# Turned attention exponents moved between quadrants: through a DRAM scratch with 5 transfers a step, or from SBUF to SBUF with 16

## Chip, cores and metric

One core of one Trainium2 chip. The metric is the time of one launch of the kernel on the device, in microseconds, as the median of several runs; smaller is better.

## The reference

Two layers over 512 latent tokens of width 2048, with 256 context tokens and adaptive normalisation. The change lies in the attention of the first layer: 12 query heads in 4 groups of 3 (one key/value head each), windows of 128 tokens on either side, the context in front, and a sink logit per head.

```python
def attend_block(args):                      # one block n of 128 queries
    n, qn = args
    kw = lax.dynamic_slice_in_dim(kp, n * BLOCK, BLOCK + 2 * WINDOW, axis=1)
    vw = lax.dynamic_slice_in_dim(vp, n * BLOCK, BLOCK + 2 * WINDOW, axis=1)
    s_win = jnp.einsum('bqkgd,bjkd->bkgqj', qn, kw).astype(jnp.float32) * scale
    s_ctx = jnp.einsum('bqkgd,bjkd->bkgqj', qn, k_ctx).astype(jnp.float32) * scale
...
    logits = jnp.concatenate([sink_logits(sink, s_win.shape[:-1]), s_ctx, s_win], axis=-1)
    p = jax.nn.softmax(logits, axis=-1)
...
    return (jnp.einsum('bkgqj,bjkd->bqkgd', p_ctx, v_ctx)
            + jnp.einsum('bkgqj,bjkd->bqkgd', p_win, vw))
```

The second product needs the probabilities with the keys on the partitions, while the first leaves the queries there. So each 128 x 128 tile of exponents has to be transposed.

## The kernel before

All products are made of three passes: both operands are split in a high part (`_hi`, made by ScalarE, ACT) and the rest (`_lo`, made by VectorE, DVE), and `three` multiplies high by high, high by low and low by high on TensorE (PE). Every matmul has line 1578, and every weight unit (512 KB, 128 x 1024) is loaded by SyncE's queue (SP, `load`, line 383), split by ACT (line 543) and DVE (line 972) and then used by PE in four banks.

**Attention.** For each of the 4 key/value heads (called heads 0 to 3 below) `attention(i)` on each engine runs through 16 slots; slots 0 to 11 hold a step k each: one query head over one block of 128 queries (block n = k // 3, query head k % 3). A step is 128 x 512 exponents for the first and last block, 128 x 640 for the others. The order on each engine is written out by hand and is that of the program:

- PE: `scores(i, k)` (it waits for `negmax_ready`, the row minimum of the step before, and in the first step of a block for the pieces of the queries), then two or three fillers, quarters of a weight unit of the gate projection; in slots 6, 9, 12 and 15 also `attend(i, n)`, the product with the values, which waits for `pt_ready` of the block's three steps.
- DVE in slot k: `maximum` (line 1265, masks the scores and takes the row minimum), `piece` (line 1238, `q_lo` for the next block's queries in slots 2, 5, 8), `turned_lo` of step k - 4 (line 1288), `turn_blocks` (line 1275), the sums' reciprocals, `lo` of a weight unit, `block_out` (line 1296, the block's values times the inverse sums, in slots 6, 9, 12, 15), and in heads 0 and 1 parts of a rotation (lines 1061 to 1065).
- ACT: `exponent` (line 744), `hi` of a weight unit, `turned_hi` of step k - 3 (line 754).
- Step 0 of heads 1 to 3 runs in slot 14 of the head before.

**The transpose.** `turn_blocks` transposes 32 x 32 blocks in place with one DVE instruction, from `probs` into one of two buffers `blocks_out` (the two parts of `cond_row`). What is left is to move blocks between the four quadrants of 32 partitions: the piece at quadrant a, quarter j has to go to quadrant j, quarter a. The SP queue does it in two trips: `store_blocks` (line 422) writes the 128 rows into the DRAM tensor `blocks`, and `fetch_blocks` (line 431) waits for that (`written`) and for a free landing buffer (`pt_ready`), and reads it back with 4 transfers, one per destination quadrant, into one of three landing buffers `blocks_in` (in `cond_row` and `modchunk`). The fetch of step k - 1 stands behind the store of step k in the queue. `turn_blocks` of step g overwrites the buffer of step g - 2, so it waits for `written` of that step:

```python
if g >= 2:
    dve.wait_ge(written[g % 2], 16 * (g // 2))
```

`turned_hi` waits for the landing of the four fetches (`pt_landed`, 64 a step).

The inverse sums of a block (128 x 3) go by `store_inverse` (line 438) to DRAM and come back broadcast over the partitions by `fetch_inverse` (line 445), 192 KB in SBUF, into one of two buffers; the fetch stands in slot 3 n + 3 and waits for `y_done` of two blocks before.

GpSimd's queue (POOL) loads in the earlier stages chunks of another weight (line 489) into `modchunk`, which is free in the attention; in the attention it only waits: its next instruction (line 519) needs the last `pt_ready`.

## Time and profile before

| | us |
|---|---|
| median of 3 runs | 1404.65 |
| lowest, highest | 1404.41, 1405.91 |
| the profiled execution | 1405.84 |
| its span | 1404.1 |
| TensorE matmul busy | 1367.9 (97%) |
| VectorE busy | 864.5 (62%) |
| ScalarE busy | 517.5 (37%) |
| GpSimd busy | 74.8 (5%) |
| mean granted TensorE clock | 0.999 |

A row of a timeline gives the start from the span's start, the duration, engine, line, operation, the names written and read, the shape, and in brackets the time for which the engine was idle before it with what ended that idle time. DMA instructions show the time that the issuing queue took, not the transfer; the time to landing is listed on its own. The attention lies from 385 to 646 us of the span.

### The profile page before, as it was taken

How to read it: one execution, taken by the hardware profiler on the slowest of the kernel's cores; microseconds unless marked ns; L12 is line 12 of the kernel's file. 1: busy time of each engine (PE TensorE's matmuls, PEld its weight loads, DVE VectorE, ACT ScalarE, POOL GpSimd, SP SyncE). 2: the span in 40 equal slices, each digit the busy share in tenths (PEclk: the TensorE clock that was granted, in tenths of full speed). 3: DMA queues.
4: the chain of work that ended last, by engine and by line, in shares of the span. 5: the costliest groups of instructions: out<-in, count | busy, mean ns of one | idle time of the engine just before them, and what ended most of it. 6: DMA issues, size and time to landing. Idle time of an engine off the chain costs nothing.

```text
span 1404.1 us, 19111 instructions
## 1 busy us (share of the span) xinstructions
PE 1367.9 (97%) x7258; PEld 1142.4 (81%) x7258; DVE 864.5 (62%) x1327; ACT 517.5 (37%) x798; POOL 74.8 (5%) x145
## 2 busy tenths in 40 slices
PE   5999999999999999999999999999999999999998
PEld 2788888888878788878888888888888888887887
DVE  6545655656787787776645776677665334474435
ACT  5323422234564645454222442212363223333332
POOL 0001111111000000000110100000000000010000
PEclk9999999999999999999999999999999999999999
DMA  9996567666676757687766666356533333365333
GB/s 384 407 396 250 180 206 254 191 186 198 201 208 163 192 172 178 176 230 261 236 198 192 195 192 194 92 173 195 160 91 102 103 91 105 105 198 181 111 90 120
DMA packets 103490, 265.35 MB, mean 189 GB/s; under 512 B 13536, under 2 KB 41200, under 8 KB 102000
## 3 DMA queue, kind: packets, MB, share of 16 engines
q1 hardware_dynamic: 81792, 185.72, 42.5%
q0 software_dynamic: 19936, 73.38, 16.7%
q10 hardware_dynamic: 1680, 5.10, 1.0%
q8 instruction: 57, 0.93, 0.3%
q14 instruction: 25, 0.20, 0.1%
HBM read 245.78 MB, written 18.38 MB: 188 GB/s over the span
## 4 chain that ended last, share of the span: by engine, by line
PE 83%; DMA 6%; DVE 5%; issue 2%; SPq 2%; ACT 2%; DVEq 0%; ACTq 0%
PE ps L1578 83%; DMA blocks<-cond_row 2%; DMA modchunk<-blocks 2%; DMA kvmem<-in_ctxT 1%; SPq L431 1%; DVE w_lo L972 1%; DVE pt_lo L1288 1%; DMA raw<-in_mod 1%; ACT w_hi L543 1%; DVE cond_row L1275 1%; DVE tmp L1265 0%; SPq L389 0%; DVE tmp L1098 0%; DVE kvmem L1160 0%; DVE kvmem L1265 0%
## 5 line engine op out<-in xcount | busy, mean ns | idle before, releaser
L1578 PE MATMUL ps<-h_hi,w_hi 128*128 128x512 f32 x1592 | 621.0, 390 | 2.1 <-DVE h_lo L1053 1.2
L1578 PE MATMUL ps<-h_lo,w_hi 128*128 128x512 f32 x1592 | 618.5, 389 | 0.0
L1578 PE MATMUL ps<-h_hi,w_lo 128*128 128x512 f32 x1592 | 618.2, 388 | 0.0
L972 DVE TENSOR_TENSOR w_lo<-raw,w_hi 128x1024 fp32r<-128x1024 f32 x206 | 252.2, 1224 | 371.2 <-ACT w_hi L543 370.3
L543 ACT CAST w_hi<-raw 128x1024 fp32r<-128x1024 f32 x206 | 216.1, 1049 | 598.8 <-PE ps L1578 598.7
L1578 PEld LDWEIGHTS ps<-h_hi,w_hi 128*128 128x128 f32 x1592 | 299.0, 188 | 65.8 <-issue 5.4
L1578 PEld LDWEIGHTS ps<-h_hi,w_lo 128*128 128x128 f32 x1592 | 298.9, 188 | 62.0
L1578 PEld LDWEIGHTS ps<-h_lo,w_hi 128*128 128x128 f32 x1592 | 299.0, 188 | 58.5
L978 DVE CUSTOM_DVE_ANT_0 modchunk<-modchunk,cond_row 128x1024 f32<-128x1024 f32 x128 | 154.6, 1219 | 19.9 <-DMA modchunk<-in_modb 19.7
L489 POOL DMA_DIRECT2D modchunk<-in_modb x128 | 67.6, 528 | 828.3 <-DVE modacc L978 811.9
L744 ACT ACTIVATE tmp<-tmp,stat 128x513 f32<-128x513 f32 (+1 forms) x24 | 18.7, 780 | 43.1 <-DVE stat L1265 43.0
L1578 PE MATMUL ps<-raw,kvmem 128*32 128x128 f32 x512 | 18.8, 293 | 15.9 <-DMA raw<-in_mod 15.7
L1578 PE MATMUL ps<-pt_hi,v_hi 128*128 128x384 f32 x72 | 25.2, 350 | 9.3 <-DVE pt_lo L1288 9.3
L1578 PE MATMUL ps<-k_hi,q_hi 128*128 128x256 f32 (+1 forms) x96 | 28.8, 300 | 2.2 <-DVE q_lo L1238 2.1
L1578 PEld LDWEIGHTS ps<-raw,kvmem 128*32 128x32 f32 x512 | 14.0, 116 | 19.8 <-issue 16.1
L744 ACT ACTIVATE kvmem<-kvmem,stat 128x513 f32<-128x513 f32 (+1 forms) x24 | 18.7, 779 | 29.3 <-DVE stat L1265 29.2
L1578 PE MATMUL ps<-k_hi,q_lo 128*128 128x256 f32 (+1 forms) x96 | 28.5, 297 | 0.0
L1578 PE MATMUL ps<-k_lo,q_hi 128*128 128x256 f32 (+1 forms) x96 | 28.4, 296 | 0.0
L1288 DVE TENSOR_TENSOR pt_lo<-modchunk,pt_hi 128x512 fp32r<-128x512 f32 (+1 forms) x32 | 23.7, 752 | 2.9 <-ACT pt_hi L754 2.9
L1275 DVE STREAM_TRANSPOSE cond_row<-tmp 128x512 f32<-128x512 f32 (+1 forms) x24 | 18.7, 779 | 10.7 <-DMA blocks<-cond_row 5.2
L1578 PE MATMUL ps<-w_hi,h_hi 128*128 128x512 f32 x64 | 24.9, 389 | 0.0
L1578 PE MATMUL ps<-w_lo,h_hi 128*128 128x512 f32 x64 | 24.9, 389 | 0.0
(231 smaller groups left out, 1356.1 us busy)
## 6 DMA issues: line engine op xcount, KB each, us to landing
raw<-in_weights SPq DMA_DIRECT2D x208, 512.0 KB, 3.6
modchunk<-in_modb POOLq DMA_DIRECT2D x128, 512.0 KB, 4.7
raw<-in_mod SPq DMA_DIRECT2D x32, 512.0 KB, 9.2
modchunk<-in_mod SPq DMA_DIRECT2D x16, 512.0 KB, 7.5
cond_row<-in_mod SPq DMA_DIRECT2D x16, 512.0 KB, 9.5
blocks<-cond_row SPq DMA_DIRECT2D x24, 320.0 KB, 5.4
blocks<-cond_row SPq DMA_DIRECT2D x24, 256.0 KB, 2.9
modchunk<-blocks SPq DMA_DIRECT2D x64, 80.0 KB, 3.6
```

What stands on the lines that cost most here:

```text
L431: sp.dma_start(blocks_in[slot][j * QUADRANT:(j + 1) * QUADRANT, 0:cols].rearrange("c (a x) -> c a x", a=4), turn_scratch[g % 4, :, j * run ...
L489: pool.dma_start(modchunk[:, slot], src).then_inc(chunk_landed[slot], 16)
L543: nc.scalar.copy(last_hi[j - HALVES] if last else w_hi[:, j % 2], src).then_inc(hi_ready, 1)
L744: nc.scalar.activation(probs[k % 2][:, 0:width], probs[k % 2][:, 0:width], ACT.Exp, bias=stat[:, 1, k % 2:k % 2 + 1], scale=-1.0, accum_ou ...
L972: nc.vector.tensor_tensor(low, src, high.bitcast(F32), ALU.subtract).then_inc(lo_ready, 1)
L978: nc.vector.tensor_tensor_reduce(out=modchunk[:, half], in0=modchunk[:, half], in1=cond_row[:, half * (D // 2):(half + 1) * (D // 2)], sca ...
L1275: nc.vector.transpose(blocks_out[g % 2][:, 0:cols].rearrange("p (j t c) -> p j t c", j=4, c=QUADRANT), probs[k % 2][:, 0:cols].rearrange(" ...
L1288: nc.vector.tensor_tensor(turned_tiles(k, pt_lo), landed_tiles(i, k), turned_tiles(k, pt_hi).bitcast(F32), ALU.subtract).then_inc(pt_ready, 1)
L1578: return nc.tensor.matmul(out, lhsT, rhs, start=start, stop=stop, skip_group_check=True)
```

## The change

Line numbers in this section are those of the kernel before unless the new file is named. The DRAM tensor `blocks` and both of its trips go. `move_blocks` (line 443 of the new file) issues 8 transfers a step on the SP queue, and POOL's queue issues the other 8 (line 532 of the new file), each from a piece of `blocks_out` (32 partitions x 128 or 160 numbers, 16 or 20 KB) directly to its place in the landing buffer. There are four landing buffers in place of three; the fourth takes the room of the two buffers of the inverse sums, which become one, placed in `kvmem`. `fetch_inverse` moves from slot 3 n + 3 to slot 3 n + 4, and waits for `y_done` of the block just before. `turned_hi` waits for both groups of 8 transfers, and `turn_blocks` of step g waits in place of `written` for all 16 transfers of step g - 2.

```diff
--- before.py
+++ after.py
@@ -138,7 +138,10 @@
 
 BLOCK_SLOTS = (6, 9, 12, 15)
 TURN_LAG = 3
-TURN_SLOTS = 3
+TURN_SLOTS = 4
+ROW_SLOT = 4
+POOL_MOVES = [(a, (a + x) % 4) for a in range(4) for x in range(2)]
+SP_MOVES = [(a, j) for j in range(4) for a in range(4) if (a, j) not in POOL_MOVES]
 NEXT_KEYS, NEXT_SCORES = 12, 14
 SWAP_SLOTS = (1, 7)
 GAINED_TILES = 3 * GROUP
@@ -228,7 +231,7 @@
         tok_stat = sb("tok_stat", [P, 2, BLOCKS], F32)
 
 
-        kv_cols = 2 * (SEQ + CTX) * KV_HEADS + 2 * SEQ
+        kv_cols = 2 * (SEQ + CTX) * KV_HEADS + 2 * SEQ + QUADRANT
         with ExitStack() as s:
             kvmem = sb("kvmem", [P, kv_cols], F32, s)
 
@@ -277,8 +280,8 @@
         chunk_flat = modchunk[:].rearrange("p a n -> p (a n)")
         most = 5 * P
         blocks_out = [cond_row[:, 0:most], cond_row[:, most:2 * most]]
-        blocks_in = [cond_row[:, 2 * most:3 * most], chunk_flat[:, 0:most], chunk_flat[:, most:2 * most]]
-        inverse_rows = [chunk_flat[:, 2 * most + b * GQA * P:2 * most + (b + 1) * GQA * P] for b in range(2)]
+        blocks_in = [cond_row[:, 2 * most:3 * most]] + [chunk_flat[:, a * most:(a + 1) * most] for a in range(3)]
+        inverse_row = kv_part(k_rope + 5 * P + QUADRANT // 2, [GQA * P])
         key_raw = kv_part(k_rope, [2, COLS])
         ctx_t = kv_part(k_keys, [KT, CTX])
         rstd_x = kv_part(k_kc, [SEQ])
@@ -315,6 +318,21 @@
         def landed_tiles(i, k):
 
             return blocks_in[(i * STEPS + k) % TURN_SLOTS][:, 0:key_tiles(k) * P].rearrange("p (a t c) -> p t a c", a=4, c=QUADRANT)
+
+        def block_source(i, k, a, j):
+
+            run = key_tiles(k) * QUADRANT
+            return blocks_out[(i * STEPS + k) % 2][a * QUADRANT:(a + 1) * QUADRANT, j * run:(j + 1) * run]
+
+        def block_target(i, k, a, j):
+
+            run = key_tiles(k) * QUADRANT
+            return blocks_in[(i * STEPS + k) % TURN_SLOTS][j * QUADRANT:(j + 1) * QUADRANT, a * run:(a + 1) * run]
+
+        def moves_landed(eng, g):
+
+            eng.wait_ge(pt_landed[g % TURN_SLOTS], 16 * len(SP_MOVES) * (g // TURN_SLOTS + 1))
+            eng.wait_ge(pt_landed_pool[g % TURN_SLOTS], 16 * len(POOL_MOVES) * (g // TURN_SLOTS + 1))
 
         S_END = 6 * 512 - 256
 
@@ -350,11 +368,11 @@
         swapped, swap_begun, piece_hi, piece_ready = sem("swapped"), sem("swap_begun"), sem("piece_hi"), sem("piece_ready")
         scores_done, negmax_ready = sem("scores_done"), sem("negmax_ready")
         exp_done, turned = sem("exp_done"), sem("turned")
-        written = [sem(f"written{i}") for i in range(2)]
         pt_landed = [sem(f"pt_landed{i}") for i in range(TURN_SLOTS)]
+        pt_landed_pool = [sem(f"pt_landed_pool{i}") for i in range(TURN_SLOTS)]
         inverse_ready = sem("inverse_ready")
         inverse_written = [sem(f"inverse_written{i}") for i in range(2)]
-        inverse_landed = [sem(f"inverse_landed{i}") for i in range(2)]
+        inverse_landed = sem("inverse_landed")
         row_stored, row_back = sem("row_stored"), sem("row_back")
         pt_hi_ready, pt_ready, pv_done, y_done = sem("pt_hi_ready"), sem("pt_ready"), sem("pv_done"), sem("y_done")
         tanh_done = sem("tanh_done")
@@ -416,21 +434,13 @@
                 sp.wait_ge(lo_ready, u + 1 - RAW_SLOTS)
                 load(weights[u], u % RAW_SLOTS)
 
-            def store_blocks(i, k):
-                g, cols = i * STEPS + k, key_tiles(k) * P
+            def move_blocks(i, k):
+                g = i * STEPS + k
                 sp.wait_ge(turned, g + 1)
-                sp.dma_start(turn_scratch[g % 4, :, 0:cols], blocks_out[g % 2][:, 0:cols]).then_inc(written[g % 2], 16)
-
-            def fetch_blocks(i, k):
-                g, cols = i * STEPS + k, key_tiles(k) * P
-                run, slot = cols // 4, g % TURN_SLOTS
-                sp.wait_ge(written[g % 2], 16 * (g // 2 + 1))
                 if g >= TURN_SLOTS:
                     sp.wait_ge(pt_ready, g + 1 - TURN_SLOTS)
-                for j in range(4):
-                    sp.dma_start(blocks_in[slot][j * QUADRANT:(j + 1) * QUADRANT, 0:cols].rearrange("c (a x) -> c a x", a=4),
-                                 turn_scratch[g % 4, :, j * run:(j + 1) * run].rearrange("(a c) x -> c a x", a=4)
-                                 ).then_inc(pt_landed[slot], 16)
+                for a, j in SP_MOVES:
+                    sp.dma_start(block_target(i, k, a, j), block_source(i, k, a, j)).then_inc(pt_landed[g % TURN_SLOTS], 16)
 
             def store_inverse(i, n):
                 b = i * BLOCKS + n
@@ -440,10 +450,10 @@
             def fetch_inverse(i, n):
                 b = i * BLOCKS + n
                 sp.wait_ge(inverse_written[b % 2], 16 * (b // 2 + 1))
-                if b >= 2:
-                    sp.wait_ge(y_done, b - 1)
-                sp.dma_start(inverse_rows[b % 2], inverse_scratch[b % 2:b % 2 + 1].rearrange("o q j -> o (q j)").broadcast_to([P, GQA * P])
-                             ).then_inc(inverse_landed[b % 2], 16)
+                if b:
+                    sp.wait_ge(y_done, b)
+                sp.dma_start(inverse_row, inverse_scratch[b % 2:b % 2 + 1].rearrange("o q j -> o (q j)").broadcast_to([P, GQA * P])
+                             ).then_inc(inverse_landed, 16)
 
             before_heads = G_Z * HALVES + 6
             load_units(1, (before_heads - HALVES) // RAW_SLOTS)
@@ -453,17 +463,13 @@
             for i in range(KV_HEADS):
                 for k in range(SLOTS):
                     if k < STEPS and (k or i == 0):
-                        store_blocks(i, k)
-                    if 1 <= k <= STEPS and (k > 1 or i == 0):
-                        fetch_blocks(i, k - 1)
+                        move_blocks(i, k)
                     if k < STEPS and k % GQA == GQA - 1:
                         store_inverse(i, k // GQA)
-                    if 3 <= k <= STEPS and k % GQA == 0:
-                        fetch_inverse(i, k // GQA - 1)
+                    if k >= ROW_SLOT and (k - ROW_SLOT) % GQA == 0 and (k - ROW_SLOT) // GQA < BLOCKS:
+                        fetch_inverse(i, (k - ROW_SLOT) // GQA)
                     if k == NEXT_SCORES and i + 1 < KV_HEADS:
-                        store_blocks(i + 1, 0)
-                    if k == NEXT_SCORES + 1 and i + 1 < KV_HEADS:
-                        fetch_blocks(i + 1, 0)
+                        move_blocks(i + 1, 0)
                     if k in UNIT_SLOTS:
                         load_unit((G_Z + i) * HALVES + UNIT_SLOTS.index(k) + 6)
                 load_unit((G_Z + i) * HALVES + HALVES + 5)
@@ -515,6 +521,15 @@
             pool.dma_start(row_scratch, cond_row[0:1]).then_inc(row_stored, 16)
             load_chunks(1, M_O * HALVES // 2)
             pool.wait_ge(row_stored, 16)
+            pool.wait_ge(acc_step, M_O * HALVES)
+            for i in range(KV_HEADS):
+                for k in range(STEPS):
+                    g = i * STEPS + k
+                    pool.wait_ge(turned, g + 1)
+                    if g >= TURN_SLOTS:
+                        pool.wait_ge(pt_ready, g + 1 - TURN_SLOTS)
+                    for a, j in POOL_MOVES:
+                        pool.dma_start(block_target(i, k, a, j), block_source(i, k, a, j)).then_inc(pt_landed_pool[g % TURN_SLOTS], 16)
             pool.wait_ge(pt_ready, KV_HEADS * STEPS)
             pool.dma_start(cond_row[:], row_scratch.broadcast_to([P, D])).then_inc(row_back, 16)
             pool.wait_ge(y_done, KV_HEADS * BLOCKS)
@@ -748,7 +763,7 @@
             def turned_hi(i, k):
 
                 g = i * STEPS + k
-                act.wait_ge(pt_landed[g % TURN_SLOTS], 64 * (g // TURN_SLOTS + 1))
+                moves_landed(act, g)
                 if k % GQA == 0 and g:
                     act.wait_ge(pv_done, g // GQA)
                 nc.scalar.copy(turned_tiles(k, pt_hi), landed_tiles(i, k)).then_inc(pt_hi_ready, 1)
@@ -1271,7 +1286,7 @@
                 g, cols = i * STEPS + k, key_tiles(k) * P
                 dve.wait_ge(exp_done, g + 1)
                 if g >= 2:
-                    dve.wait_ge(written[g % 2], 16 * (g // 2))
+                    moves_landed(dve, g - 2)
                 nc.vector.transpose(blocks_out[g % 2][:, 0:cols].rearrange("p (j t c) -> p j t c", j=4, c=QUADRANT),
                                     probs[k % 2][:, 0:cols].rearrange("p (t j c) -> p j t c", j=4, c=QUADRANT)).then_inc(turned, 1)
 
@@ -1292,10 +1307,10 @@
 
                 b = i * BLOCKS + n
                 dve.wait_ge(pv_done, b + 1)
-                dve.wait_ge(inverse_landed[b % 2], 16 * (b // 2 + 1))
+                dve.wait_ge(inverse_landed, 16 * (b + 1))
                 nc.vector.tensor_tensor(main[:, i * GQA + FG:(i + 1) * GQA + FG, n * P:(n + 1) * P],
                                         ps[:, 7, P:512].rearrange("p (j q) -> p j q", j=GQA),
-                                        inverse_rows[b % 2].rearrange("p (q j) -> p j q", j=GQA), ALU.mult).then_inc(y_done, 1)
+                                        inverse_row.rearrange("p (q j) -> p j q", j=GQA), ALU.mult).then_inc(y_done, 1)
 
             def attention(i):
 
@@ kernel() @@
-    blocks = nc.dram_tensor("blocks", (4, P, 5 * P), F32, kind="Internal").ap()
```

**The queue of SyncE (SP), steps 3 and 4 of head 0.** Names: `blocks` is the DRAM scratch, `cond_row` holds `blocks_out` and one landing buffer, `modchunk` the other landing buffers. Before:

```order
L422 DMA blocks<-cond_row 128x640 [waits turned]
L431 DMA modchunk<-blocks 32x4x128 [waits written0]
L431 DMA modchunk<-blocks 32x4x128 x3
L445 DMA modchunk<-inverses 128x384 [waits inverse_written0]
L422 DMA blocks<-cond_row 128x640 [waits turned]
L431 DMA cond_row<-blocks 32x4x160 [waits pt_ready,written1]
L431 DMA cond_row<-blocks 32x4x160 x3
L383 DMA raw<-in_weights 128x1024 [waits lo_ready]
```

and with the change:

```order
L443 DMA modchunk<-cond_row 32x160 [waits turned]
L443 DMA modchunk<-cond_row 32x160 x7
L443 DMA cond_row<-cond_row 32x160 [waits pt_ready,turned]
L443 DMA cond_row<-cond_row 32x160 x7
L455 DMA kvmem<-inverses 128x384 [waits inverse_written0]
L401 DMA raw<-in_weights 128x1024 [waits lo_ready]
```

Five issues a step have become eight on this queue, the fetch behind the next step's store is gone, and the inverse sums' fetch now stands behind the moves of step 4. POOL's queue holds the same two rows a step (line 532) and nothing else between them.

**VectorE (DVE), steps 3 and 4 of head 0.** `L1265 ISA` is the masked minimum, STREAM_TRANSPOSE is `turn_blocks`. Before:

```order
L1265 ISA tmp,stat<-ps,masks,tmp 128x640 [waits scores_done,sink_placed]
L1265 ISA stat 128x1
L1275 STREAM_TRANSPOSE cond_row<-tmp 128x640 [waits written1,exp_done]
L1061 TENSOR_TENSOR scratch<-scratch,rope 128x512 [waits swapped]
L1265 ISA kvmem,stat<-ps,masks,kvmem 128x640 [waits scores_done,sink_placed]
L1265 ISA stat 128x1
L1288 TENSOR_TENSOR pt_lo<-cond_row,pt_hi 128x4x128 [waits pt_hi_ready]
L1275 STREAM_TRANSPOSE cond_row<-kvmem 128x640 [waits written0,exp_done]
L972 TENSOR_TENSOR w_lo<-raw,w_hi 128x1024 [waits hi_ready]
L1063 TENSOR_TENSOR main<-main,rope 128x512
L1065 TENSOR_TENSOR main<-main,scratch 128x512 [waits own]
L1265 ISA tmp,stat<-ps,masks,tmp 128x640 [waits scores_done,sink_placed]
```

and with the change, where the two transposes stand at the same places in the same order:

```order
L1290 STREAM_TRANSPOSE cond_row<-tmp 128x640 [waits pt_landed_pool1,pt_landed1,exp_done]
L1076 TENSOR_TENSOR scratch<-scratch,rope 128x512 [waits swapped]
L1280 ISA kvmem,stat<-ps,masks,kvmem 128x640 [waits scores_done,sink_placed]
L1280 ISA stat 128x1
L1303 TENSOR_TENSOR pt_lo<-cond_row,pt_hi 128x4x128 [waits pt_hi_ready]
L1290 STREAM_TRANSPOSE cond_row<-kvmem 128x640 [waits pt_landed_pool2,pt_landed2,exp_done]
```

No instruction of DVE, ACT or PE has moved; the transposes wait for the landing of two steps before in place of the store of two steps before.

## Rows read from the trace of the kernel before

**Rows 1.** The page, busy time of PE: busy us, share of the span, instructions.

```profile
PE 1367.9 (97%) x7258; PEld 1142.4 (81%) x7258; DVE 864.5 (62%) x1327; ACT 517.5 (37%) x798; POOL 74.8 (5%) x145
```

**Rows 2.** Busy time over the four heads, 385 to 646 us: sum of the windows.

```profile
sum 261.00, PE 249.47 PEld 214.25 DVE 195.37 ACT 137.98 POOL 0.00; mean PE 62.37 PEld 53.56 DVE 48.84 ACT 34.49 POOL 0.00
```

**Rows 3.** Who waited for whom, 380 to 660 us: total, times, longest.

```profile
PE ps L1578 <- DVE pt_lo L1288: 9.3, 10, 1.7
ACT pt_hi L754 <- DMA modchunk<-blocks: 9.2, 7, 2.9
...
DVE cond_row L1275 <- DMA blocks<-cond_row: 5.2, 4, 2.9
...
PE ps L1578 <- DVE q_lo L1238: 2.1, 3, 0.9
```

**Rows 4.** Timeline of PE: one wait each in heads 0 and 1, the last in heads 2 and 3.

```profile
420.91 0.45 PE L1578 MATMUL ps<-pt_hi,v_hi 128*128 128x384 f32 x1 [1.00 <-DVE pt_lo L1288]
...
469.91 0.44 PE L1578 MATMUL ps<-k_hi,q_hi 128*128 128x384 f32 x1 [0.89 <-DVE q_lo L1238]
...
567.42 0.44 PE L1578 MATMUL ps<-pt_hi,v_hi 128*128 128x384 f32 x1 [1.30 <-DVE pt_lo L1288]
...
635.20 0.45 PE L1578 MATMUL ps<-pt_hi,v_hi 128*128 128x384 f32 x1 [1.21 <-DVE pt_lo L1288]
```

**Rows 5.** Timeline of DVE: transposes of step 0 of heads 1, 2, 3.

```profile
447.08 0.70 DVE L1275 STREAM_TRANSPOSE cond_row<-kvmem 128x512 f32<-128x512 f32 x1
...
513.53 0.70 DVE L1275 STREAM_TRANSPOSE cond_row<-kvmem 128x512 f32<-128x512 f32 x1
...
579.91 0.70 DVE L1275 STREAM_TRANSPOSE cond_row<-kvmem 128x512 f32<-128x512 f32 x1
```

**Rows 6.** Timeline of POOL: three issues in a row.

```profile
124.86 0.54 POOL L504 DMA_DIRECT2D masks<-in_masks  x1
125.39 1.06 POOL L489 DMA_DIRECT2D modchunk<-in_modb  x2
```

**Rows 7.** Line 489, its 128 chunk loads on POOL: ns minimum, median, maximum.

```profile
L489 POOL DMA_DIRECT2D modchunk<-in_modb x128: 527/527/552, 125.4 to 1296.5; - x128
```

**Rows 8.** Timeline of SP: four fetches of one step.

```profile
463.09 2.00 SPq L431 DMA_DIRECT2D modchunk<-blocks  x4
```

**Rows 9.** DMA issues: KB each, median us from issue to landing.

```profile
modchunk<-inverses SPq DMA_DIRECT2D x16, 192.0 KB, 5.0
...
mod_v<-in_edges POOLq DMA_DIRECT2D x1, 32.0 KB, 2.1
```

**Rows 10.** All fetches from and stores to the tensor `blocks`: time to landing.

```profile
DMA to landing us min/median/max: 1.8/3.6/9.8
```

**Rows 11.** Timeline of DVE: transposes of steps 0 and 2 of head 0.

```profile
386.06 0.71 DVE L1275 STREAM_TRANSPOSE cond_row<-kvmem 128x512 f32<-128x512 f32 x1 [0.89 <-ACT kvmem L744]
...
391.51 0.71 DVE L1275 STREAM_TRANSPOSE cond_row<-kvmem 128x512 f32<-128x512 f32 x1 [0.41 <-ACT kvmem L744]
```

**Rows 12.** Timeline of DVE: head 1, transposes of steps 1 to 4, `q_lo`, step 6.

```profile
455.11 0.71 DVE L1275 STREAM_TRANSPOSE cond_row<-tmp 128x512 f32<-128x512 f32 x1
...
457.74 0.71 DVE L1275 STREAM_TRANSPOSE cond_row<-kvmem 128x512 f32<-128x512 f32 x1
...
461.79 0.84 DVE L1275 STREAM_TRANSPOSE cond_row<-tmp 128x640 f32<-128x640 f32 x1 [0.99 <-ACT tmp L744]
...
465.00 0.84 DVE L1275 STREAM_TRANSPOSE cond_row<-kvmem 128x640 f32<-128x640 f32 x1 [0.38 <-ACT kvmem L744]
...
469.31 0.55 DVE L1238 TENSOR_TENSOR q_lo<-main,q_hi 128x384 fp32r<-128x384 f32 x1
...
473.16 0.84 DVE L1275 STREAM_TRANSPOSE cond_row<-kvmem 128x640 f32<-128x640 f32 x1 [0.39 <-ACT kvmem L744]
```

**Rows 13.** Timeline of DVE: after `block_out` in head 1, after step 3's transpose in head 2.

```profile
477.67 0.88 DVE L1265 CUSTOM_DVE_ANT_0 tmp<-ps,masks,tmp 128x640 f32<-128x640 f32 x1 [1.64 <-PE ps L1578]
...
529.36 0.89 DVE L1265 CUSTOM_DVE_ANT_0 kvmem<-ps,masks,kvmem 128x640 f32<-128x640 f32 x1 [0.64 <-PE ps L1578]
```

4 lines of the change are left out of this document (2 added, 2 removed).

## Prediction

> **What bounds the kernel now.** I read the busy times first: TensorE (PE) is busy for 1367.9 of 1404.1 us [rows 1], so what a change elsewhere can give is idle time of PE. The windows over the four heads, where the whole change lies, bound it: 261.0 us, of which PE is busy for 249.5 [rows 2]. All of the idle time that this stage has is 11.5 us. The waits say who ends it: `pt_lo` of DVE 9.3 us in 10 waits, `q_lo` of DVE 2.1 us in 3 [rows 3]; no DMA stands there. Behind them ACT's `pt_hi` waited 9.2 us in 7 waits for fetches (one more, for the buffer in `cond_row`, cost it some 3 us), and DVE's transpose 5.2 us for the store of two steps before [rows 3]. The question is how much of this came through to PE.
>
> Very little. Nearly all of these DMA waits lie in heads 2 and 3, and head 1 has hardly any; yet from step 0 to step 0, head 1 lasts 513.53 - 447.08 = 66.45 us and head 2 579.91 - 513.53 = 66.38 us [rows 5]. What can be traced through is the wait before `attend(i, 2)` in heads 2 and 3, 1.30 and 1.21 us [rows 4], where `pt_hi` had stood waiting for its fetch just before; heads 0 and 1 have no such wait. The other eight waits for `pt_lo` recur in every head with no late DMA ahead of them: DVE takes the row minimum of the scores that PE has just made, and only then the `pt_lo` that PE wants next. So the transfers own 2.5 us of PE's time, and the order of DVE owns the other 9.
>
> The sum is made against the profiled execution, 1405.84 us (span 1404.1), which is 1.2 us over the median of the runs, 1404.65; a difference found in the trace is applied to the median. About 0.2%, 2.8 us, is what a measurement of this kernel can tell from no change.
>
> **Term 1: the removed DRAM trip, -2.5 us.** A step went by a store, then four fetches that queued behind the next step's store; now one trip does. The two waits of 1.30 and 1.21 us go [rows 4]. Bounds: nothing, if another instruction is late there; 3.9 us, if the early landing also brings the waits before `attend(i, 1)` in heads 1 and 3, up to 1.7 us [rows 3], down to the 1.00 us of head 0 [rows 4]. I take 2.5, the part that can be traced.
>
> **Term 2: the issues.** POOL: two loads in a row take 1.06 us, and the one before starts 0.53 earlier [rows 6]; all 128 chunk loads take 527 to 552 ns [rows 7]. So 8 moves take 8 x 0.53 = 4.24 us, the last starting 3.71 us after the first. SP: four fetches take 2.00 us [rows 8], about 0.48 each, so 8 moves take 3.9 us; it no longer waits between a store and a fetch, but still issues 8 weight loads and 8 transfers of inverse sums per head. POOL is the slower half, and all 16 have to land. Neither queue delays PE by itself; both set when a step has landed.
>
> **Term 3: the wait in front of the transpose, +5.5 us.** Before, step g's transpose needed the store of step g - 2, one issue right behind the transpose. Now it needs the last of 16 moves. What a small transfer takes from issue to landing, no row shows for quadrant to quadrant. Nearest: 1.8 us, the fastest store or fetch, and 3.6 us, their median, most of them behind a store of 256 or 320 KB [rows 10]; 2.1 us, a 32 KB load issued by POOL [rows 9]. I take 2.2, nearest to the POOL row, since no store stands ahead any more. A step then lands 3.71 + 2.2 = 5.9 us after its transpose, plus what POOL still owes for the step before.
>
> Head 1 [rows 12]: the transpose of step 1 ends at 455.82, its last move starts at 459.53 and lands at 461.7; step 3's transpose, at 461.79, just gets by. Step 2's transpose ends at 458.45, but POOL is free at 460.06, so its last move starts at 463.77 and lands at 465.97; step 4's transpose stood at 465.00, so it waits 0.97 us. Head 0 starts with three steps close together: step 0's transpose ends at 386.77, its moves land at 392.68, and step 2's transpose, at 391.51 [rows 11], waits 1.17 us. The same arithmetic carried on gives 0.19 for step 3 and 0.80 for step 4, 2.16 in all. In heads 2 and 3, steps 1 and 2 are 2.2 us apart and the waits come to 0.3 us before step 3 and 1.2 before step 4.
>
> What stands behind a waiting transpose: on DVE a `w_lo`, two rotations (heads 0 and 1) or two `h_lo` (head 3), the row minimum of step 5, and `q_lo`, which ends at 469.86 in head 1 [rows 12]; PE starts its scores at 469.91, after waiting 0.89 us for just that [rows 4]. From the transpose's end at 465.84 to the start of `q_lo` at 469.31 DVE runs these one right behind the other. There is no cover: a wait of step 4's transpose reaches PE whole in heads 0, 1 and 3. Step 3's does too in heads 0 and 1, through the minimum and exponent of step 4; in heads 2 and 3 DVE has 0.64 us to spare there, since it waits for PE's scores [rows 13]. In head 2, without a rotation, about 0.5 us is covered before `q_lo`, but step 5's transpose adds some. Waits from step 6 on (`pt_lo`, `block_out` follow) are covered: DVE idles 1.64 us for PE after the first `block_out` [rows 13]. On PE: 2.16 + 0.97 + 1.2 + 1.19 = 5.5 us. With 1.8 us to landing the same chains give 3.6, with 3.6 us 10.8; these are the bounds.
>
> **Term 4: the inverse sums, +0.3 us.** Their fetch now stands in SP's queue behind the moves of step 4. In head 2 eight-issue trains of 3.9 us from 522.3 on put it at about 538.8; with the 5.0 us that it took before [rows 9] it lands at 543.8, some 2 us after `block_out` wants it, against the 1.64 us of cover [rows 13]. In the other heads the delay is 1.0 or less, inside the cover. Nothing to 2 us; I take 0.3.
>
> The rest costs nothing: the fourth landing buffer only removes waits on `pt_ready`; POOL had nothing to do in this stage (0.00 busy) [rows 2]; `pt_hi` of step g stands three slots after the transpose, some 11 us or more, against 6 to 8 to landing.
>
> **Sum:** -2.5 + 5.5 + 0.3 = +3.3 us, so 1404.65 + 3.3 = **1408.0 us**.
>
> The 128 loads of POOL keep their 527 ns although DVE runs two-input instructions beside them [rows 7]. The Trainium skill, SBUF — State Buffer, section "SBUF: two separate sides", holds that descriptors of a transfer issued from GpSimd can't be written while DVE runs an instruction in a two-port mode, and names fp32 copies; the rows so far speak against a price here, and the case is the third rival below. The skill's DMA: Bandwidth & Descriptors, section "Anatomy of one DMA — SWDGE (gpsimd) path", gives about 2.0 us fixed plus bytes over 436 GB/s, so 2.05 us for 20 KB; by that, as an estimate, term 3 would be 4.8 in place of 5.5. That agrees with the row of 2.1 us.
>
> **Rivals.**
>
> *Faster (18%).* The moves land at least as early as DVE wants them and term 1 is all that is left. The point: for step 4 in head 1, POOL issues 15 intervals after 455.82 before the last move, so 15 c + L must be at most 465.00 - 455.82 = 9.18 us. With L = 2.2 that needs issues of c = 0.465 us in place of 0.53; rows 6 and 7 show none below 0.527. With c = 0.53 it needs L = 1.2, below the fastest landing of all [rows 10]. If it holds: 1404.65 - 2.5 = 1402.2, or 1400.8 with term 1's upper bound.
>
> *No difference (34%).* The same mechanism with landings of 1.8 us (+3.6 - 2.5 = +1.1, 1405.8), or a stall of DVE that PE makes up in waits that it had anyway. For it: head 2, where DVE stalls, the longest of 2.9 us [rows 3], made the head no longer [rows 5]. Against it: those lie in steps 9 to 11, where DVE has room; the new ones lie in steps 2 to 4, where it has none. That the change removes a trip which was hidden anyway belongs here.
>
> *POOL's issues take longer (10%).* The rows show at most three issues in a row, each for a load [rows 6]; eight moves in a row beside a DVE that is three quarters busy (195.4 of 261.0 us) [rows 2] may take longer. The steps 1 to 6 of head 1 follow each other every (473.16 - 455.11) / 5 = 3.6 us [rows 12]. At c = 0.65 a train takes 5.2 us; step 4's last move then starts 31 issues after 455.82, at 476.0, and lands at 478.2, and step 6's transpose waits 5.0 us, of which some 1.6 are covered: +3.4 us per head, 13.6 in all, and 1404.65 - 2.5 + 13.6 + 0.3 = 1416.1 us. At c = 1.0 POOL bounds the heads, 12 x 8 = 96 us against 66.4, and four times 29.6 gives some 1523 us; this has 3 of the 10%. It is the case to watch, since from 0.53 on each tenth of a microsecond an issue costs several in all. By the rule on descriptor writing it would come out this way.
>
> **How the numbers follow.** The forecast's case has 38%, no difference 34%, faster 18%, POOL slower 10%. Slower by over 0.2% is 38 + 10 = 48%. The time of the likeliest case is 1408.0. The range reaches from 1401.5 (below term 1 alone, so that most of the faster case is inside) to 1416.0 (term 3 at its upper bound, +10.8 - 2.5 + 2 = +10.3, and some more); outside are about 7% above and 8% below. The forecast's own range is 1407.5 to 1415.
>
> **What would show it.** Right: PE's waits for `q_lo` in heads 0, 1 and 3 grow from 2.1 us in total to some 5; DVE's transposes wait for moves in steps 2 to 4, some 5 to 7 us in total; `pt_hi` waits for no DMA; POOL issues 384 moves of about 0.53 us; PE has no wait before `attend(i, 2)`. Wrong: POOL rows other than 0.53 us, landings under 1.5 or over 3.6 us, transposes that never wait, or waits on them with no longer wait on PE.

## The result, and the profile after it

| | before | after |
|---|---|---|
| median, us | 1404.65 | 1471.30 (1470.52 to 1472.37) |
| ratio of the times | | 1.0473, 95% interval 1.0455 to 1.0491 |
| the profiled execution, its span | 1405.84, 1404.1 | 1470.52, 1468.8 |
| TensorE (PE) busy, us | 1367.9 | 1393.7 |
| PE idle (span less busy), us | 36.2 | 75.1 |
| mean granted TensorE clock | 0.999 | 0.980 |

The change costs 66.7 us, or 4.7%, nearly all of it in the four heads: from the last `block_out` to the end both executions take the same 755 us. The idle time of PE grew by 38.9 us and its busy time by 25.8 us, for the same 7258 matmuls; together 64.7, the growth of the span.

The page, busy times (us, share of the span, instructions), beside [rows 1]:

```profile
PE 1393.7 (95%) x7258; PEld 1162.1 (79%) x7258; DVE 863.0 (59%) x1327; ACT 517.3 (35%) x798; POOL 263.5 (18%) x529
```

DVE and ACT do what they did before in the same time. POOL has some 190 us of issues more, 498 ns each.

The waits of 380 to 730 us (engine, what waited, what it waited for: us in total, times, longest), beside [rows 3]:

```profile
DVE cond_row L1290 <- DMA modchunk<-cond_row: 50.6, 17, 5.3
...
PE ps L1593 <- DVE pt_lo L1303: 33.2, 11, 4.4
DVE main L1311 <- DMA kvmem<-inverses: 24.4, 8, 9.4
...
DVE cond_row L1290 <- issue: 13.8, 6, 3.6
...
PE ps L1593 <- DVE q_lo L1253: 9.5, 4, 2.9
...
DVE cond_row L1290 <- DMA cond_row<-cond_row: 4.2, 1, 4.2
...
ACT pt_hi L769 <- DMA modchunk<-cond_row: 2.2, 2, 1.3
```

Line 1290 is `turn_blocks`, which writes `cond_row`: it waits 68.6 us in 24 of 48 steps (three lines, 50.6 + 13.8 + 4.2) for the transfers of two steps before, where it had waited 5.2 us in 4. The line with "issue" names no transfer, but in all six of its waits the transpose starts 0.08 or 0.09 us after SP's last move of two steps before has landed, so they are the same wait. Line 1311 is `block_out`, which waits another 24.4 us for the inverse sums. `pt_hi`, which the removed trip had held up for some 13 us (9.2 in [rows 3], and one wait of 3.5 for the buffer in `cond_row`), waits 2.2. So the wait moved from the reader of the landed data to the writer of the next ones, and from 18 us in both it grew to 71. PE's waits for `pt_lo` and `q_lo` came to 42.7 us, from 11.4; three smaller ones that it did not have before (3.4 us for `block_out`, 2.8 for the row minimum, 1.4 for `w_lo`) make up the rest of the 38.9.

The issues on the two queues (name, number: ns minimum/median/maximum of one), beside [rows 7, 8]:

```profile
L443 SPq DMA_DIRECT2D modchunk<-cond_row x288: 507/591/3140, 392.9 to 700.1; - x144
L443 SPq DMA_DIRECT2D cond_row<-cond_row x96: 507/591/1669, 387.8 to 681.4; - x96
```

```profile
L532 POOL DMA_DIRECT2D modchunk<-cond_row x288: 496/498/512, 392.8 to 696.4; - x144
L532 POOL DMA_DIRECT2D cond_row<-cond_row x96: 496/498/518, 388.3 to 678.0; - x96
```

POOL never takes more than 518 ns. SP's median is 591 ns, and the starts of its issues lie 0.63 us apart, so a train of 8 takes 4.94 to 5.08 us. In 11 of the 48 trains it takes longer, up to 7.5 us, because single issues take up to 3.14; before, single fetches took up to 2.0. What holds those up is not shown. The timeline of SP shows the queue behind its work (start, us, last number: how many issues the row holds):

```profile
484.63 0.43 SPq L401 DMA_DIRECT2D raw<-in_weights  x1
485.16 4.95 SPq L443 DMA_DIRECT2D modchunk<-cond_row  x8
490.21 6.05 SPq L443 DMA_DIRECT2D cond_row<-cond_row  x8
496.36 0.53 SPq L455 DMA_DIRECT2D kvmem<-inverses  x1
496.93 0.44 SPq L401 DMA_DIRECT2D raw<-in_weights  x1
```

The eight transfers that start at 485.16 belong to step 3 of head 1, whose transpose had ended at 481.03 (first row below). They sat 4.1 us in the queue behind those of step 2, a store of sums and a weight load; the last one starts at 489.5 and lands near 494. Only then can step 5's transpose run. The timeline of DVE, steps 3, 4 and 5 of head 1 (in brackets the idle time before), beside [rows 12]:

```profile
480.18 0.85 DVE L1290 STREAM_TRANSPOSE cond_row<-tmp 128x640 f32<-128x640 f32 x1 [1.31 <-DMA modchunk<-cond_row]
...
485.36 0.85 DVE L1290 STREAM_TRANSPOSE cond_row<-kvmem 128x640 f32<-128x640 f32 x1 [2.34 <-DMA modchunk<-cond_row]
...
494.26 0.85 DVE L1290 STREAM_TRANSPOSE cond_row<-tmp 128x640 f32<-128x640 f32 x1 [3.75 <-DMA modchunk<-cond_row]
```

And so PE, in its own timeline: it waits for the `q_lo` and then for the `pt_lo` that stand behind those transposes, beside [rows 4]:

```profile
489.97 0.45 PE L1593 MATMUL ps<-k_hi,q_hi 128*128 128x384 f32 x1 [2.94 <-DVE q_lo L1253]
...
491.18 0.63 PE L1593 MATMUL ps<-h_lo,w_hi 128*128 128x512 f32 x1
491.61 0.63 PE L1593 MATMUL ps<-h_hi,w_lo 128*128 128x512 f32 x1
...
496.60 0.69 PE L1593 MATMUL ps<-pt_hi,v_hi 128*128 128x384 f32 x1 [3.08 <-DVE pt_lo L1303]
```

The matmuls of 128 x 512 in between start 0.43 us apart. The windows of 3 us over this place say why (window, us, PE busy, granted clock, share of the DMA engines, GB/s):

```profile
484.00:487.00 3.00, 3.00 (x15) 1.00 0.50 55
487.00:490.00 3.00, 0.07 (x2) 1.00 0.62 218
490.00:493.00 3.00, 3.00 (x12) 0.69 0.69 83
493.00:496.00 3.00, 0.52 (x2) 0.50 0.11 28
496.00:499.00 3.00, 2.40 (x7) 0.50 0.26 66
499.00:502.00 3.00, 3.00 (x11) 0.60 0.85 289
502.00:505.00 3.00, 3.00 (x17) 1.00 0.40 68
```

PE stood idle for 2.94 us, and about a microsecond after it had started again the granted clock fell from its upper level (1.00, 2.4 GHz) to the lower one (0.50, 1.2 GHz), until some 501 us. Before, no stretch of the attention had less than 1.00. Over the attention:

```profile
385.00:460.00 75.00, 62.93 (x285) 0.91 0.40 98
460.00:540.00 80.00, 66.26 (x300) 0.89 0.49 107
540.00:620.00 80.00, 69.93 (x320) 0.91 0.49 107
620.00:710.00 90.00, 79.15 (x376) 0.96 0.52 130
```

Worked out from these four rows, with only the two levels to choose from, 2 x (1 - clock) x length gives 14 + 18 + 14 + 7 = 53 us at 0.50; one more stretch, 713.0 to 719.9 us, lies behind them. Laid over the eleven stretches at 0.50 themselves, the windows add up to this:

```profile
sum 58.03, PE 48.61; mean PE 4.42
```

PE was busy for 48.6 of these 58.0 us and did half the work in them that it does at 1.00, so 24 us were lost: nearly all of the 25.8 us of added busy time. A long pause is paid a second time. Of the 13 pauses of 2.0 us or more in the attention, eleven have such a stretch beginning in them or at most 1.5 us behind them, one lies inside a stretch, and one of 2.63 us brought none. The shorter ones brought none either, as before the change, where the longest was 1.7 us.

The chain of the whole execution that ended last had been PE 83%, DMA 6%. Now (by engine, then by line):

```profile
PE 74%; SPq 15%; DVE 4%; DMA 4%; issue 2%; ACT 1%; DVEq 0%; ACTq 0%
```

SP's issues, an engine that moves no data itself, hold 15% of the execution; in 387 to 480 us line 443 alone has 70.3% of that chain.

### The profile page after: what moved, and what is told of

The parts are those of the page before. It is cut to its first block, busy times and chain, and to the rows that moved or that the text cites. A ratio compares the mean times of both kernels' runs of the same rounds, so it can differ in the third digit from the quotient of the medians.

```text
span 1468.8 us, 19716 instructions
## 1 busy us (share of the span) xinstructions
PE 1393.7 (95%) x7258; PEld 1162.1 (79%) x7258; DVE 863.0 (59%) x1327; ACT 517.3 (35%) x798; POOL 263.5 (18%) x529
## 4 chain that ended last, share of the span: by engine, by line
PE 74%; SPq 15%; DVE 4%; DMA 4%; issue 2%; ACT 1%; DVEq 0%; ACTq 0%
PE ps L1593 74%; SPq L443 13%; DMA kvmem<-in_ctxT 1%; DMA kvmem<-inverses 1%; DMA modchunk<-cond_row 1%; DVE w_lo L987 1%; DVE tmp L1113 1%; DMA inverses<-inverse 1%; SPq L401 1%; SPq L448 0%; DVE cond_row L1290 0%; SPq L407 0%; DVE main L1117 0%; DVE pt_lo L1303 0%; DVE kvmem L1175 0%
## 5 line engine op out<-in xcount | busy, mean ns | idle before, releaser
L532 POOL DMA_DIRECT2D modchunk<-cond_row x288 | 141.2, 498 | 79.6 <-DVE cond_row L1290 73.4
L1593 PE MATMUL ps<-pt_hi,v_hi 128*128 128x384 f32 x72 | 31.3, 435 | 33.3 <-DVE pt_lo L1303 33.2
L532 POOL DMA_DIRECT2D cond_row<-cond_row x96 | 47.1, 498 | 52.5 <-DVE cond_row L1290 52.0
L1593 PEld LDWEIGHTS ps<-pt_hi,v_hi 128*128 128x128 f32 x72 | 17.6, 244 | 39.1 <-DVE pt_lo L1303 38.9
L769 ACT CAST pt_hi<-modchunk 128x512 fp32r<-128x512 f32 (+1 forms) x36 | 23.7, 665 | 51.6 <-PE ps L1593 49.4
L1290 DVE STREAM_TRANSPOSE cond_row<-kvmem 128x512 f32<-128x512 f32 (+1 forms) x24 | 18.7, 777 | 30.5 <-DMA modchunk<-cond_row 12.7
L1593 PEld LDWEIGHTS ps<-k_hi,q_hi 128*128 128x128 f32 x96 | 18.5, 193 | 17.1 <-DVE q_lo L1253 11.2
```

Source lines behind the costliest of these rows:

```text
L532: pool.dma_start(block_target(i, k, a, j), block_source(i, k, a, j)).then_inc(pt_landed_pool[g % TURN_SLOTS], 16)
L769: nc.scalar.copy(turned_tiles(k, pt_hi), landed_tiles(i, k)).then_inc(pt_hi_ready, 1)
L1290: nc.vector.transpose(blocks_out[g % 2][:, 0:cols].rearrange("p (j t c) -> p j t c", j=4, c=QUADRANT), probs[k % 2][:, 0:cols].rearrange(" ...
L1593: return nc.tensor.matmul(out, lhsT, rhs, start=start, stop=stop, skip_group_check=True)
```

## Experiments

Each was measured once, beside an execution of the kernel before in the same sequence on the same chip (1402.8 to 1408.0 us from chip to chip, so that differences, not times, are compared; ten executions on one chip ranged from 1403.3 to 1405.6, so a difference of two single executions says little below some 3 us); the one that was timed in rounds, before_pool_fetch, has its interval. In the texts written ahead of the first four runs, A is that the trains of moves on SP and POOL are too long for two buffers, B a cause that fewer moves would hardly help, and C the single row for the inverse sums; later texts say what their letters mean. "Moves" are the transfers of `move_blocks`; "8 + 8" is the number on SP and on POOL. The runs whose names begin with moves_ or end in _little, wide_8 and sp_from_dram leave out or misplace a part of the data and serve for their times alone. The table stands first, the reasons behind it:

| run | moves SP + POOL | us | over before | PE busy | PE idle |
|---|---|---|---|---|---|
| the change | 8 + 8 | 1471.30 | 66.7 | 1393.7 | 75.1 |
| three_out | 8 + 8 | 1469.73 | 66.9 | 1389.3 | 78.8 |
| inverse_two | 8 + 8 | 1469.72 | 66.9 | 1393.4 | 74.7 |
| both_rooms | 8 + 8 | 1465.77 | 61.2 | 1391.2 | 72.9 |
| inverses_pool | 8 + 8 | 1451.85 | 47.3 | 1386.0 | 64.2 |
| split_6_10 | 6 + 10 | 1457.44 | 49.5 | 1380.1 | 75.5 |
| relieved | 7 + 9 | 1424.46 | 19.9 | 1375.9 | 46.7 |
| sp_from_dram | 8 + 8 | 1429.94 | 22.0 | 1379.7 | 48.6 |
| moves_12 | 6 + 6 | 1429.47 | 26.7 | 1379.4 | 48.4 |
| moves_12_4_8 | 4 + 8 | 1429.50 | 21.5 | 1376.1 | 51.8 |
| moves_12_5_7 | 5 + 7 | 1413.53 | 8.6 | 1372.3 | 39.5 |
| moves_10 | 5 + 5 | 1411.20 | 6.2 | 1370.9 | 38.6 |
| moves_8 | 4 + 4 | 1406.53 | 3.7 | 1370.4 | 34.4 |
| wide_8 | 4 + 4, all bytes | 1407.84 | -0.2 | 1369.1 | 37.1 |
| after_little | 8 + 8 | 1460.74 | 53.9 | 1389.8 | 69.3 |
| moves_12_4_8_little | 4 + 8 | 1415.95 | 9.1 | 1373.5 | 40.8 |
| relieved_little | 7 + 9 | 1420.28 | 13.4 | 1372.8 | 45.6 |
| before_little | none | 1402.56 | -4.3 | 1366.7 | 34.2 |
| before_pool_fetch | none | 1407.62 | 3.1 | 1368.2 | 37.0 |

### Fewer moves: moves_12 and moves_8

```diff
-SP_MOVES = [(a, j) for j in range(4) for a in range(4) if (a, j) not in POOL_MOVES]
+SP_MOVES = [(a, j) for j in range(4) for a in range(4) if a != j and (a, j) not in POOL_MOVES]   # moves_12, POOL 6
+SP_MOVES = [(a, (a + 2) % 4) for a in range(4)]                                                  # moves_8, POOL 4
```

> Leaves out the 4 moves of a step that stay in their own quadrant (their places in the landing buffers keep old numbers); 6 moves on each queue are left. Theory A (the rate of the first queue): in the changed kernel a move takes the first queue 0.59 us and 0.04 to the next, 4.96 us a step against some 3.6 us between transposes; with 6 the train is 3.7 us. The chain of trains, landings and transposes of two steps on, worked out with the rows of the kernel before and 0.62 us a move, then gives 3 to 5 us of waits of the transposes in place of 36 to 39, and no lowered TensorE clock: 1405 to 1411 us. Theory B (the trip itself, some 2.5 us from the last issue to landing, is what the transposes wait for, however many moves there are): 1455 to 1470 us. Theory C (the single buffer of the inverse sums and its later place in the queue are the cause): no more than 5 us off, 1465 to 1471.

> Leaves out half of the moves of a step: 4 on each queue, the destinations one and two quadrants on. Theory A: the trains take 2.5 us, no transpose waits at all; the time is that of the kernel before less the 2.5 us that its transfers own, 1401 to 1404 us. Theory B: 1450 to 1468 us. Theory C: 1465 to 1471.

26.7 and 3.7 us over the kernel before. moves_12 lies between A and the other two, moves_8 2.5 us above A. The loss hangs on the moves and grows much faster than their number: 4 + 4 leave hardly any, though the transposes still wait for moves in place of a store and there is still one row for the inverse sums.

### More room: three_out, inverse_two, both_rooms

A third buffer `blocks_out` from head 1 on, in keys that are no longer needed; a second row for the inverse sums, fetched a slot earlier; both.

```diff
-return blocks_out[(i * STEPS + k) % 2][a ...]
+return blocks_out[out_slot(i * STEPS + k)][a ...]      # three from head 1 on
-ROW_SLOT = 4
+ROW_SLOT = 3                                           # and inverse_rows[row_of(b)]
```

> All 16 moves, 8 and 8, but from head 1 on the transposes have three buffers to write (the third lies in the keys of heads 0 and 1, which are used up by then), so that each waits for the moves of three steps before. Theory A with the chain over two buffers (it is the rate of the first queue that ends late, but the transposes' wait two steps on that hands it to PE): the same arithmetic gives 10.5 us of waits in head 0 and about 3 us in each other head, 20 us in place of 36 to 39, and less of the lowered clock: 1425 to 1445 us. If the first queue's rate alone bounds the heads (12 trains of 4.96 us and 16 other issues, 68 us a head against 66.4 before), heads 1 to 3 last 68 to 70 us each. If neither buffers nor rate but the landing counts: 1465 to 1471.

> The changed kernel with two buffers for the inverse sums again (the second in the keys of head 0), waited for as before, and their fetch back in slot 3 n + 3. Theory C: block_out waited 24.4 us for this fetch; if that is of its own making, some 10 to 25 us come back: 1446 to 1462 us. Theory A: the fetch is late because it stands behind trains of 4.96 us, and the fetch a slot earlier saves little: 1464 to 1472 us.

> The changed kernel with both rooms at once: a third buffer for turned exponents from head 1 on and a second row for the inverse sums (fetch one slot earlier). Theory A (SP's queue has too much to issue: 12 trains of 4.95 us, 8 inverse transfers and 8 weight loads come to 69 to 70 us a head where a head took 66.4): both waits fall, but heads still last 69 to 71 us and the total is 1418 to 1445. Theory B (some wait always takes the place of the last one, with no room for gain in buffers at all): 1463 to 1472. Theory C (only the two rooms were missing): 1402 to 1410.

No gain from either, 5 us from both. For three_out theory A had 1425 to 1445, which missed by 25 us; inverse_two came out as A had it. In three_out the transposes waited 37 us in place of 69 (28.0 below, and 5.6 and 3.7 in two more lines), but `block_out` took it over (waits of 380 to 730 us):

```profile
DVE main L1317 <- DMA kvmem<-inverses: 68.7, 14, 9.9
...
DVE cond_row L1296 <- DMA modchunk<-cond_row: 28.0, 6, 6.8
...
PE ps L1599 <- DVE stat L1286: 22.0, 9, 5.2
```

With both rooms the same lateness was spread over the transposes (47.4 us), `pt_hi` (49.7) and `block_out` (35.9). I had expected 1418 to 1445 there, from SP's load over a whole head (70 us for 66.4). That was the wrong mean: of a head's 12 trains 11 lie in slots 1 to 11, a step every 3.6 to 4.4 us, where SP needs 4.95 us for the moves and some 0.7 for the rest, and slots 12 to 15 have only one. More room lets it fall further behind; it doesn't give it time.

### Relieving SP: inverses_pool, split_6_10, relieved

inverses_pool issues `store_inverse` and `fetch_inverse` on POOL; split_6_10 only splits the moves otherwise; relieved has both rooms, the inverse transfers on POOL and 7 + 9 moves.

```diff
 # SP's loop in inverses_pool
-if k < STEPS and k % GQA == GQA - 1:
-    store_inverse(i, k // GQA)
-if k >= ROW_SLOT and (k - ROW_SLOT) % GQA == 0 and (k - ROW_SLOT) // GQA < BLOCKS:
-    fetch_inverse(i, (k - ROW_SLOT) // GQA)
```

> The changed kernel with only the store and the fetch of the inverse sums moved from SP's queue to POOL's. SP then has 12 x 4.95 + 8 x 0.45 = 63 us a head, POOL 12 x 3.92 + 8 x 0.5 = 51. Theory A (load of SP's queue) expects a clear gain, 1430 to 1455, since SP gets under the 66.4 us of a head, while two buffers still make transposes wait. Theory B (the chain from one transpose over its moves to the transpose two steps later, whatever else is queued) expects 1462 to 1471.

> The changed kernel, complete, with 6 of the 16 transfers on SP and 10 on POOL. Theory D: SP has 6 x 0.62 + 0.7 = 4.4 us a step, POOL 10 x 0.49 = 4.9, both above the 3.6 to 4.4 us between steps, where the change has 5.7 and 3.9: 1435 to 1458, better than the change by what the slower queue gained (5.7 to 4.9), and still far above the kernel before. Theory E: 1465 to 1475.

> Everything that theory A names at once: third buffer from head 1 on, second inverse row, inverse transfers on POOL, and the moves split 7 on SP (4.3 us a step) and 9 on POOL (4.4 us a step). SP has 56 us a head, POOL 57. Theory A expects heads of 66 to 67 us again from head 1 on and a total of 1400 to 1410, with the granted clock back at 0.99 or more. If the 16 small transfers cost something beside their issue (ports, DMA engines, a slower DVE), it stays at 1425 or more.

Taking a mere 8 transfers a head from SP gives 19 us back, two moves a step 17, all together 47. So SP's queue carries most of the loss. But relieved didn't get to the 1400 to 1410 expected, although its mean load was some 56 us a head on either queue: in the dense stretch SP still needs 7 x 0.63 us and, every second step, a weight load, 4.7 us a step, and from 469.3 to 484.6 us its timeline has no gap over 0.1 us. An estimate from the two issue times says that sixteen moves are too many for these two queues however they are split: together they issue 1 / 0.63 + 1 / 0.49 = 3.6 moves a microsecond, so 4.4 us a step at best, before anything else is issued. A third queue was not tried.

### What an issue costs: sp_from_dram, wide_8

SP's moves read a DRAM input of the same shape in place of SBUF; and 8 moves of 64 partitions, which carry all the bytes of a step.

```diff
-sp.dma_start(block_target(i, k, a, j), block_source(i, k, a, j))
+sp.dma_start(block_target(i, k, a, j), rope_rows(i, k, a, j))                          # sp_from_dram
-return blocks_out[...][a * QUADRANT:(a + 1) * QUADRANT, j * run:(j + 1) * run]
+return blocks_out[...][a * 64:(a + 1) * 64, j * run:(j + 1) * run]                     # wide_8
```

> The changed kernel, where SP's 8 transfers of a step read 32 x 160 numbers from a DRAM input in place of the turned exponents (the right data do not come over); number, size, target and semaphores are the same. If the source in SBUF is what makes an issue of SP 0.62 us long where the fetches before took 0.50, the median of the line falls to 0.43 to 0.50 us, a train to 4 us and the total to 1420 to 1445. If SP needs that for any transfer of this size or number, the rows stay at 0.59 and the total at 1465 to 1475.

> The changed kernel with 8 transfers a step of 64 partitions x 128 or 160 numbers, 4 on each queue: all bytes of a step are moved from SBUF to SBUF, but half to half of the partitions instead of quadrant to quadrant, so the pieces do not end where the product needs them. Theory D (price per transfer on SP's queue, in the dense stretch): SP's trains 2.4 to 2.6 us, POOL's 2.0, and 1403 to 1410, like moves_8 with half of the bytes. If the price goes by bytes or rows, the issues become twice as long and it stays above 1440.

The rows of SP's issues in sp_from_dram:

```profile
L447 SPq DMA_DIRECT2D modchunk<-in_rope x288: 310/422/1515, 391.9 to 662.3; - x144
L447 SPq DMA_DIRECT2D cond_row<-in_rope x96: 310/422/557, 388.3 to 644.0; - x96
```

From DRAM the same issue takes SP 422 ns, from SBUF 591. Nor is it the source in SBUF alone: `store_blocks` of the kernel before reads SBUF, too, and writes DRAM. And the price falls on what stands directly behind a move as well, as the store of the inverse sums shows, before and after (it is 422 ns in sp_from_dram):

```profile
L422 SPq DMA_DIRECT2D blocks<-cond_row x48: 319/338/1312, 386.9 to 632.7; - x48
...
L438 SPq DMA_DIRECT2D inverses<-inverse x16: 430/430/488, 394.6 to 636.6; - x16
```

```profile
L448 SPq DMA_DIRECT2D inverses<-inverse x16: 579/581/591, 403.7 to 700.8; - x16
```

So SP is slow at issuing from SBUF to SBUF, and at what comes next. With the source in DRAM the change would lose 22.0 us, not 66.7. In wide_8 an issue of twice the rows took 597 ns on SP and 523 on POOL, and the time was, as far as single executions tell, that of the kernel before. The price goes by the transfer, and hardly by bytes or rows.

### Not the rate of one queue alone: moves_12_4_8, and the weight loads

```diff
-POOL_MOVES = [(a, (a + 1) % 4) for a in range(4)] + [(0, 2), (1, 3)]     # moves_12
+POOL_MOVES = [(a, (a + x) % 4) for a in range(4) for x in (1, 2)]        # moves_12_4_8, SP has 4
```

> The changed kernel without the four diagonal pieces (as in moves_12: a part of the data is not brought over), but with 4 of the 12 on SP and 8 on POOL in place of 6 and 6. The total of transfers, bytes and the wait of the transpose are those of moves_12 (1429.5); only the queues differ: SP 4 x 0.62 + 0.7 = 3.2 us a step, POOL 8 x 0.49 = 3.9, where steps 1 to 11 follow each other every 3.6 to 4.4 us. Theory D (in the dense stretch, slots 1 to 11, SP's queue falls behind with every step; the mean over a head is not what counts): 1404 to 1414. Theory E (it is the number of small transfers, on whichever queue): 1425 to 1433.

Here theory D fell: SP had room (3.2 us a step), and it was still 21.5 us over the kernel before. The transposes (DVE's timeline, steps 1 to 4 of head 1) show the place:

```profile
463.29 0.71 DVE L1290 STREAM_TRANSPOSE cond_row<-tmp 128x512 f32<-128x512 f32 x1
...
465.92 0.71 DVE L1290 STREAM_TRANSPOSE cond_row<-kvmem 128x512 f32<-128x512 f32 x1
...
469.97 0.84 DVE L1290 STREAM_TRANSPOSE cond_row<-tmp 128x640 f32<-128x640 f32 x1 [0.99 <-ACT tmp L759]
...
477.44 0.84 DVE L1290 STREAM_TRANSPOSE cond_row<-kvmem 128x640 f32<-128x640 f32 x1 [4.64 <-DMA modchunk<-cond_row]
```

and the transfers issued from 464 to 478 us (number, KB each, median us to landing) the cause:

```profile
raw<-in_weights SPq DMA_DIRECT2D x1, 512.0 KB, 6.7
modchunk<-cond_row POOLq DMA_DIRECT2D x16, 16.0 KB, 1.7
modchunk<-cond_row POOLq DMA_DIRECT2D x8, 20.0 KB, 4.5
modchunk<-cond_row SPq DMA_DIRECT2D x8, 16.0 KB, 1.8
modchunk<-cond_row SPq DMA_DIRECT2D x4, 20.0 KB, 5.7
```

POOL issues the 16 moves of steps 1 and 2 without a gap from 464.29, so the last starts at 471.6. In between, at 469.73, SP issues a weight load of 512 KB, which lands 6.7 us later, at 476.4. One by one, POOL's moves up to 469.2 landed after 1.6 to 1.9 us; the last four of step 2, from 469.66 on, took 5.1 to 6.1, and landed between 474.7 and 477.3, about when the load did. SP's four of step 3, from 470.84 on, took 5.5 to 5.9. So it happens on POOL's queue as well as on SP's, and step 4's transpose, at 477.44, waits for the last of them. (The Trainium skill, DMA: Bandwidth & Descriptors, section "Queues, rings and completion order", says that a completion signal is written only after all earlier writes of its DMA engine, whichever queue they came from. These rows fit it.) To see what that is worth, the 32 weight loads of the attention were cut to 8 KB:

```diff
-load_unit((G_Z + i) * HALVES + UNIT_SLOTS.index(k) + 6)
+load_little((G_Z + i) * HALVES + UNIT_SLOTS.index(k) + 6)
 # in load_little, for the unit u:
+sp.dma_start(raw[:, u % RAW_SLOTS].rearrange("p a n -> p (a n)")[:, 0:16], weights[u][:, 0:16]).then_inc(...)
```

> The kernel before with the 32 weight loads of the attention cut from 128 x 1024 to 128 x 16 numbers (the rest of each unit is not brought in; issues and semaphores stay). It is the floor for the next three. Every theory expects 1401 to 1405: nothing of PE's time in the attention hung on the loads but the 2.5 us of term 1.

> The changed kernel with the same 32 weight loads cut to 8 KB. Theory F (a small transfer that is issued while a weight load is under way lands only with it, 4 to 6 us after issue in place of 1.7 to 2.1): a good part of the loss goes, 1415 to 1440, and what stays is the rate of SP's issues (8 x 0.62 + 0.7 us a step). Theory D (issues alone): 1460 to 1472.

> moves_12_4_8 (diagonal pieces left out, 4 on SP, 8 on POOL; 1429.5 us) with the same weight loads cut to 8 KB. Theory F: SP needs 3.2 and POOL 3.9 us a step and transfers land after 2 us, so 1402 to 1410. Theory E (number of transfers): 1425 to 1433 as before.

> The relieved version (all 16 transfers, 7 on SP and 9 on POOL, three buffers, two inverse rows, inverse transfers on POOL; 1424.5 us) with the same weight loads cut to 8 KB. Theory F with D's rates (SP 5.0 us a step, POOL 4.5 to 5.0, against steps of 3.6 to 4.4 in slots 1 to 11, three buffers to fall behind on): 1404 to 1415. Issues alone: 1420 to 1425.

Against the floor before_little, the change loses 58.2 us in place of 66.7, moves_12_4_8 13.4 in place of 21.5, relieved 17.7 in place of 19.9. Theory F is true of the landings (the median of a move fell from 2.6 to 2.0 us on SP and from 2.8 to 1.7 on POOL, the change against after_little) and explains 2 to 9 us, more than a third of the loss in moves_12_4_8, but only an eighth in the change. All three of my ranges by theory F were too low: 1415 to 1440 for after_little, 1402 to 1410 for moves_12_4_8_little (1416.0) and 1404 to 1415 for relieved_little. after_little and relieved_little came out where the issues alone had put them.

### Both together: moves_12_5_7, moves_10

The prediction had set up the rule for this place itself: step 4's transpose needs the moves of steps 1 and 2, so (2n - 1) c + L must be at most 9.2 us, the time from the end of step 1's transpose to the start of step 4's. Here n is the number of moves of a step on one queue, c the time from one issue to the next and L the landing of the last. With the slower queue's n and c as measured, the issue part is 9.45 us for the change, 9.3 for split_6_10 (POOL), 6.9 for moves_12 (SP), 7.35 for moves_12_4_8 and for sp_from_dram (POOL, in both), 4.4 for moves_8 and wide_8.

```diff
+SP_MOVES = [(a, (a + 3) % 4) for a in range(4)] + [(0, 2)]               # both runs
+POOL_MOVES = [(a, (a + x) % 4) for a in range(4) for x in (1, 2) if (a, x) != (0, 2)]   # moves_12_5_7
+POOL_MOVES = [(a, (a + 1) % 4) for a in range(4)] + [(1, 3)]             # moves_10
```

> moves_12 (diagonal pieces left out) with 5 transfers on SP and 7 on POOL. Theory G, issue train and landing together on the slower queue: (2n - 1) c is 9 x 0.63 = 5.7 us on SP and 13 x 0.49 = 6.4 on POOL, where 6 and 6 has 6.9 on SP (26.7 us over the kernel before in the same call) and 4 and 8 has 7.35 on POOL (21.5 over). It expects less than both: 12 to 20 us over the kernel before. Theory E (the number of transfers): 21 to 27 over.

> The changed kernel with 10 of the 16 transfers, 5 on each queue (the diagonal and two more pieces are left out). (2n - 1) c is 5.7 us on SP, 4.4 on POOL; with a weight load ahead 5.7 + 5.7 = 11.4 against 9.2. Theory G: 6 to 16 us over the kernel before in the same call, between moves_8 (3.7 over, 4.4 us of issues) and moves_12. Theory E: by the number alone some 14 over, so this run alone does not tell G from E; it tells how the loss grows.

8.6 and 6.2 us over. The same twelve transfers cost 26.7, 21.5 or 8.6 us by how they are split, the least where the slower queue's part (6.4 us) is least: the number of transfers is not the cause (theory E), the slower queue's train is. The gain was larger than the 12 to 20 expected. Set in order of the issue part: 0 to 4 us of loss at 4.4, 6 at 5.7, 9 at 6.4, 27 at 6.9, 21.5 and 22.0 at 7.35, 49.5 at 9.3, 67 at 9.45. It jumps between 6.4 and 6.9 us; by the rule alone, with a landing of 2 us, it would at 7.2, where nothing is left of the 9.2. sp_from_dram and moves_12_4_8, with 16 and 12 moves but the same train on POOL, lose the same. So the rule sorts the splits roughly, and does not give the losses. Why moves_12 lies above moves_12_4_8 in spite of a shorter train is open; in it SP also carries the inverse transfers and weight loads among the moves.

### A version that might beat both: before_pool_fetch

The kernel before, with the four fetches of a step from DRAM issued by POOL.

```diff
-                    if 1 <= k <= STEPS and (k > 1 or i == 0):
-                        fetch_blocks(i, k - 1)
+            for i in range(KV_HEADS):          # on POOL's queue, with the same waits
+                for k in range(STEPS):
+                    fetch_blocks(i, k)
```

> The kernel before with one edit: the four fetches of a step from DRAM are issued by POOL, the store stays on SP. The trip through DRAM stays, but no fetch queues behind the next store. If term 1 of the prediction is right (the transfers owned 2.5 us of PE's time, the waits of 1.30 and 1.21 us before attend(i, 2)), it gains 1 to 2.5 us: 1401.5 to 1404 against 1404.65. If PE makes that up elsewhere, no difference. If POOL's issue of 128 pieces takes much over 0.53 us, it is slower.

Slower by 0.3%: ratio 1.0028, interval 1.0016 to 1.0039. The 1 to 2.5 us of gain did not come. POOL's issues took 552 ns, `pt_hi` waited longer for its fetches than before (9.2 us there), though PE did not wait longer for `pt_lo` (9.3 there):

```profile
ACT pt_hi L755 <- DMA modchunk<-blocks: 16.0, 10, 3.4
...
PE ps L1579 <- DVE pt_lo L1289: 8.6, 10, 1.8
```

The store in front of the fetches remained (POOL waited 133.5 us for it). The place of the fetch in SP's queue had cost next to nothing: before, the first fetch of a step starts 0.1 us (median of the 48 steps) after its store has landed. It is the landing of the store that is long, 4.9 us. And from POOL the four fetches take longer, 6.9 us in place of 5.0 from the first issue to the last landing. So the median step lands 11.7 us after its transpose, in place of 11.4. No complete version that was tried beats the kernel before.

## Why the prediction was wrong

Predicted 1408.0 us (1401.5 to 1416.0), measured 1471.3. The direction had the largest chance, 48%; the size is far outside the range.

**Term 1, -2.5 us: right in size, as far as it can be seen.** It can't be read from the change, where later waits cover the place. In before_little the weight loads no longer delay the trips, PE's waits for `pt_lo` fall from 9.3 [rows 3] to 6.3 us and its idle time by 2.0. That late transfers owned 2 to 3 us of PE's time fits this single execution; before_pool_fetch, which was meant to gain them, did not bring its fetches in earlier and so does not test it.

**Term 2 is the step that failed, at "SP: ... about 0.48 each, so 8 moves take 3.9 us" and "POOL is the slower half".** POOL needed 0.49 us a move, 3.92 a train, less than the 4.24 assumed. SP needed 0.63, 4.94 to 5.08 a train, and more in 11 of 48; in all 48 steps SP's last move landed after POOL's, by 2.2 us in the median. The 0.48 came from four fetches from DRAM [rows 8]; sp_from_dram shows that an issue with that source is short in the new kernel too (422 ns), and one from SBUF to SBUF is not. I bounded the landing of an SBUF-to-SBUF transfer from both sides, as no row showed one, and took the issue of the same unseen operation as known. The rival "issues take longer" had the mechanism and nearly the price (c = 0.65 on POOL: 1416.1), but put it on the wrong queue. On SP it is worse than on POOL, since SP also issues the inverse transfers and the weight loads, which the sum of term 2 named and did not add to the step: 4.95 + 0.7 us against steps of 3.6. For POOL, with nothing else, 0.65 would have meant 5.2.

**Term 3, +5.5 us: the right place, mis-sized.** Predicted were transposes that wait in steps 2 to 4 of a head, 5 to 7 us in total; measured 68.6 us in 24 of 48 steps. By its rule, with c = 0.63, step 4 needs 9.45 + L against 9.2: late by the whole landing time, in every head (it waited 2.2, 2.3, 3.0 and 2.9 us), and the backlog is handed on to the steps behind, which the term had called covered. The landing itself was taken as 2.2 us, "since no store stands ahead any more": the fastest took 1.6, the medians were 2.6 (SP) and 2.8 (POOL), and the slowest 7.0, since 8 weight loads a head are still ahead. The stores before took 2.0 to 8.4 us behind those same loads and were rarely late, because one transfer, issued at once, had the whole time of two steps for it; the last of 8 has what 8 issues leave.

**Term 4, +0.3 us:** `block_out` waited 24.4 us for the fetch of the inverse sums (8 times, up to 9.4). The term had the place in the queue right and timed it with trains of 3.9 us and no backlog. inverses_pool, where that fetch leaves SP's queue, gives 19 us back, though part of that is the time SP gains for its moves.

**Not in the sum at all: the clock.** PE's waits were priced one for one. The 38.9 us of idle time brought 25.8 us of busy time with them, through 58.0 us at 0.50. Before, the granted clock had been 0.999 and the longest wait for `pt_lo` or `q_lo` 1.7 us [rows 3], so no row of before showed the price; a bound from both sides (nothing, or a matmul stretch at half speed behind each long wait) would have shown that 1416 was no upper end.

**"The rest costs nothing"** held: `pt_hi` hardly waits for moves (2.2 us), the fourth landing buffer and POOL's work cost nothing seen, DVE is no slower beside POOL's issues (863.0 against 864.5 us busy). What the third rival feared, issues of POOL that get longer beside DVE, did not show: they stayed at 496 to 518 ns throughout.

**Of the rivals:** "faster" and "no difference" fell at SP's issue price: both needed trains under 9.2 us less a landing. moves_8 and wide_8 (3.7 us over and 0.2 under) show that "no difference" would about have come true with half as many issues. "Faster" did not show in any version with moves.

## What to carry to other kernels

Replacing a few large transfers by many small ones is priced in issues: take the price of one for the very source, target and queue in question, add everything else that the queue issues, and compare it with the spacing of the steps in the dense stretch, not with the mean over a period. Where a buffer is reused, ask for the last transfer of the train and let it land behind the largest load that is under way. And a wait of TensorE of 2 to 4 us may cost more than its length, through the clock: here each microsecond of added idle time brought 0.3 (split_6_10) to 0.7 us (the change) of added busy time. So a sum of waits is a lower end.

## What the runs showed of the hardware

- An issue of a 16 to 20 KB move of 32 partitions from SBUF to SBUF takes SP 591 ns (0.63 us from start to start), from DRAM to SBUF 422 ns, and what is issued directly behind such a move is slow, too (581 ns for a store of 1.5 KB in place of 430, 580 for a weight load in place of 430); POOL needs 498 ns. 64 partitions cost 597 and 523 ns, so nearly the same for twice the bytes. What in SP makes it so was not found, nor what holds up single issues for 1 to 3 us. The Trainium skill, DMA: Bandwidth & Descriptors, section "Issuing engines are not separate DMA queues", holds that issuing on several engines at once saves only the time of issue, "which is usually small relative to the DMA itself". Here the time of issue was the bound: 4.95 us of it a step on SP, for moves that land in 2 us where nothing delays them.
- A small transfer issued while a 512 KB load was under way landed at about the same time as the load, 4 to 6 us after its issue instead of 1.7, on either queue. One case has no load to explain it: the last move of the very first train landed 4.0 us after issue in the change and 3.5 in after_little, and gave the first stall. The one transfer beside the moves that the profile has there is an instruction fetch, a packet of 16 KB (at 393.5 us, 1.2 us behind the move's issue; at 392.8 in after_little). That it holds the move up is not shown.
- After a pause of PE of 2.94 us, and 1 us of work, the granted clock stood at 0.50 until about 501 us, some 10 us, with a second pause of 3.08 us inside; matmuls of 128 x 512 started 0.43 us apart. The cost is not proportional to idle time: split_6_10 and the change had 75 us idle each, with 34 and 58 us at 0.50 in the attention, of which PE was busy for 19.5 and 48.6, and 12.2 and 25.8 us of added busy time.
